# Which engine sums the conditioning products, in what order the weight halves are made, and which products are split in three

## The reference, cut to what matters

```python
for l in range(2):
    mod = (silu(c) @ w_ada[l] + b_ada[l])           # six vectors of 2048: sh1 sc1 g1 sh2 sc2 g2
    h = rms_norm(x) * (1 + sc1) + sh1
    z = h @ w_in[l]     # differential attention q, k, v; latent q_a, kv_a, k_rope; gate u, v
    out_a = diff_attention(...)                     # 6 heads, chunk mask, ALiBi
    out_b = latent_attention(...)                   # 6 heads, through w_uq and w_ukv
    out_c = spatial_gating(...)
    x = x + g1 * (concat(out_a, out_b, out_c) @ w_out[l])
    h = rms_norm(x) * (1 + sc2) + sh2
    x = x + g2 * conv_ffn(h)     # up to 2 x 5632 columns, 3-tap conv, silu gate, down to 2048
```

## Time and profile before

| | |
|---|---|
| three runs | 2524.81, 2528.46 (median), 2529.74 us |
| the profiled execution | 2523.4 us, its span 2521.6 us |
| TensorE matmul busy | 2422.4 us, 96% |
| VectorE busy | 1796.8 us, 71% |
| ScalarE busy | 1122.5 us, 45% |
| GpSimd busy | 536.5 us, 21% |
| granted TensorE clock, mean | 0.975 |

### The profile page before, as it was taken

The page is one execution under the profiler, slowest core; times in us unless marked ns, Lnnn a source line. Parts: engine busy times, 40 slices in busy tenths (PEclk is TensorE's granted clock), DMA queues, the critical chain, the costliest instruction groups (busy, mean ns, idle before and its releaser), DMA issues.

```text
span 2521.6 us, 37553 instructions
## 1 busy us (share of the span) xinstructions
PE 2422.4 (96%) x15080; PEld 2025.7 (80%) x15080; DVE 1796.8 (71%) x2477; ACT 1122.5 (45%) x1549; POOL 536.5 (21%) x565
## 2 busy tenths in 40 slices
PE   6799999989999999999999999999999999999999
PEld 2578778768888888888878888777888888888888
DVE  2455657987668889989986477788766566665765
ACT  2233555345443454445444355534544344443543
POOL 3332310132322133213330120002231002200220
PEclk8899999999999999999999999999999999999999
DMA  9999886677779888898787677556776556555654
GB/s 311 340 300 313 263 265 205 207 244 242 252 257 316 277 257 266 295 297 253 255 267 230 202 234 219 180 170 210 243 247 213 185 187 188 184 187 188 185 185 149
DMA packets 450509, 596.86 MB, mean 237 GB/s; under 512 B 24172, under 2 KB 397984, under 8 KB 450080
## 3 DMA queue, kind: packets, MB, share of 16 engines
q1 hardware_dynamic: 394640, 392.47, 49.1%
q0 software_dynamic: 55296, 201.35, 24.4%
q10 hardware_dynamic: 400, 0.65, 0.1%
HBM read 592.30 MB, written 2.10 MB: 236 GB/s over the span
## 4 chain that ended last, share of the span: by engine, by line
PE 85%; DVE 6%; DMA 3%; issue 3%; ACT 2%; POOL 0%; ACTq 0%; DVEq 0%; SPq 0%; POOLq 0%
PE bank L1029 85%; DMA ada<-in_w_ada_dram 3%; DVE wlo L1594 1%; ACT whi L1351 1%; DVE acc L1588 1%; DVE xT L1632 1%; DMA rows<-in_b_ada_dram 0%; DVE r L1651 0%; DVE T L1666 0%; DVE hx L1687 0%; ACT hx L1418 0%; PE bank L1320 0%; DMA raw<-in_w_in_dram 0%; ACT sq L1404 0%; DVE xT L1633 0%
## 5 line engine op out<-in xcount | busy, mean ns | idle before, releaser
L1029 PE MATMUL bank<-hx,whi 128*128 128x512 f32 (+1 forms) x3968 | 1365.6, 391 | 4.1 <-DVE hx L1689 4.1
L1594 DVE TENSOR_TENSOR wlo<-raw,whi 128x1024 fp32r<-128x1024 f32 (+1 forms) x774 | 936.6, 1216 | 593.9 <-ACT whi L1351 592.6
L1351 ACT ACTIVATE whi<-raw 128x1024 fp32r<-128x1024 f32 (+1 forms) x774 | 785.3, 1019 | 1118.2 <-PE bank L1029 1093.7
L1029 PE MATMUL bank<-hx,wlo 128*128 128x256 f32 x3840 | 1096.5, 286 | 31.2 <-DVE hx L1687 10.8
L1029 PEld LDWEIGHTS bank<-hx,whi 128*128 128x128 f32 x3968 | 744.7, 190 | 165.6 <-DVE hx L1689 4.8
L1029 PEld LDWEIGHTS bank<-hx,wlo 128*128 128x128 f32 x3840 | 733.5, 191 | 62.7 <-issue 25.1
L1029 PE MATMUL bank<-mx,whi 128*128 128x512 f32 x1728 | 618.5, 400 | 0.0
L1029 PE MATMUL bank<-mx,wlo 128*128 128x256 f32 x1728 | 495.5, 287 | 2.7 <-DVE wlo L1594 1.2
L983 POOL DMA_DIRECT2D ada<-in_w_ada_dram x384 | 253.9, 664 | 1135.5 <-DVE acc L1588 581.9
L1029 PEld LDWEIGHTS bank<-mx,whi 128*128 128x128 f32 x1728 | 329.6, 191 | 76.1
L1029 PEld LDWEIGHTS bank<-mx,wlo 128*128 128x128 f32 x1728 | 331.6, 192 | 15.4 <-issue 10.6
(11 more groups left out here) (163 smaller groups left out, 1326.6 us busy)
## 6 DMA issues: line engine op xcount, KB each, us to landing
ada<-in_w_ada_dram POOLq DMA_DIRECT2D x384, 512.0 KB, 6.3
raw<-in_ffn_w_up_dram SPq DMA_DIRECT2D x352, 512.0 KB, 4.5
raw<-in_ffn_w_down_dram SPq DMA_DIRECT2D x176, 512.0 KB, 4.0
raw<-in_w_in_dram SPq DMA_DIRECT2D x128, 512.0 KB, 5.4
raw<-in_w_out_dram SPq DMA_DIRECT2D x48, 512.0 KB, 4.8
raw<-in_w_out_dram SPq DMA_DIRECT2D x32, 256.0 KB, 3.1
raw<-in_mla_w_uq_dram SPq DMA_DIRECT2D x12, 384.0 KB, 4.2
raw<-in_mla_w_ukv_dram SPq DMA_DIRECT2D x6, 512.0 KB, 4.9
```

Source lines behind the costliest of these rows:

```text
L1029: return pe.matmul(out_, lhsT, rhs, start=start, stop=stop, skip_group_check=True)
L1351: return act.activation(out_, in_, ACT.Copy)
L1594: i_ = tt(dst, src, high.bitcast(F32), ALU.subtract)
```

## The change

- `VECTOR_HALVES` replaces `VECTOR_BATCHES`: halves 4, 10 to 19, 22 and 23, that is the first half of batch 2, and batches 5, 6, 7, 8, 9 and 11. Batches 4 and 10 go to TensorE, and so does the second half of batch 2, as before.
- The spreading of batches over slots: batch 1 over 16 slots (was 14); layer 0's batch 2 over 36 slots, then batches 3 and 4 from pair 14 of the late pairs (they were 2, 3 and 4 over 70); layer 1's batch 9 over 36 slots, then batch 10 from pair 10 (they were 9 and 10 over 94).
- `three` in place of `paired` for the w_in pairs 9 to 13 (all that are neither `TWO_PAIRS` nor `TOKEN_PAIRS`), for all of w_out, and for the last pair of the last down pass of each layer. Their `copy` goes to ScalarE; their `addz` and `res` are one VectorE instruction where they were two.
- `place_splits` puts `av`, and `prob` whose `exp` came earlier, between `hi` and `lo`.
- `transition` issues the three products of the norm itself, and one burst between the first and the second, another behind `inv`, if the next batch is TensorE's.
- Small moves in the queues: `dak` in three groups, a free slot ahead of a group in layer 1, the latent items ahead of the gate's in `out_projection` and one empty slot fewer there, `inv` of the latent queries one group earlier.

```diff
-VECTOR_BATCHES = (4, 6, 7, 8, 10)
+VECTOR_HALVES = (4, 10, 11, 12, 13, 14, 15, 16, 17, 18, 19, 22, 23)
+LAST_DOWN = (len(PASS_BLOCKS) - 1, 7)
+TWO_PAIRS = DAQ_PAIRS + DAK_PAIRS
+SPREAD_FROM = (SGV_PAIRS[0], QA_PAIRS[1])
     def vector_next(self):
-        return self.ada_g // 8 in VECTOR_BATCHES
+        return self.ada_g // 4 in VECTOR_HALVES
-                self.ada_over(2, len(order) - 6)
+                self.ada_over(2, len(order) - 4)
...
-        if l == 0:
-            self.ada_over(5, 18 + 30 + 22)
-        else:
-            self.ada_over(11, 28 + 30 + 24 + 12)
+        self.ada_over(3 if l == 0 else 10, 36)
...
+            if pair == SPREAD_FROM[l]:
+                self.ada_over(5 if l == 0 else 11, 4 * len(LATE_PAIRS[LATE_PAIRS.index(pair):]) - 2 + 24 + 10)
...
+        for kind in ("T", "H", "L"):
+            for k in range(2):
+                self.add(kind, l, "kva", k)
         self.steps.extend([("sg", l, 0), ("sg", l, 1), ("Tsg", l, 0), ("Tsg", l, 1)])
...
-        q.extend([[], [("krgain", l)], [("ukvjob", l, 0)] + qa[0],
+        q.extend([[("krgain", l)], [("ukvjob", l, 0)] + qa[0],
...
         self.drain()
+        self.add("ms", l, j, 0)
+        spare = not self.vector_next()
+        if spare:
+            self.burst()
+        self.add("ms", l, j, 14)
+        self.add("ms", l, j, 15)
         self.add("root", l, j)
         self.add("inv", l, j)
-        if not self.vector_next():
+        if spare:
             self.burst()
...
+            steps.extend(own[:n])
+            own = own[n:]
+            ready = [x for x in own if x[0] == "av" or (x[0] == "prob" and ("exp", *x[1:]) not in own)]
+            splits(None, ready)
+            steps.extend(x for x in own if x not in ready)
...
+                            elif x_.what == "win" and x_.i not in TWO_PAIRS:
+                                i_ = three(b[:, 0:S], wh, wl, hi(hx, k), lo(hx, k), start, stop)
                             elif x_.what == "wout":
-                                i_ = paired(b, wh, wl, mixed(k), start, stop)
+                                i_ = three(b[:, 0:S], wh, wl, mixed(k)[:, 0:S], mixed(k)[:, S:2 * S], start, stop)
+                            elif x_.what == "down" and (x_.b, x_.i) == LAST_DOWN:
+                                i_ = three(b[:, 0:S], wh, wl, hi(mx, k), lo(mx, k), start, stop)
...
-                    order.after(stt(xa, b[:, S:2 * S], g, xa, ALU.mult, ALU.add))
+                        if (ph, pair) != LAST_DOWN:
+                            order.after(stt(xa, b[:, S:2 * S], g, xa, ALU.mult, ALU.add))
                     stt(xa, b[:, 0:S], g, xa, ALU.mult, ALU.add).then_inc(emptied_dve, 1)
```

More of the change, by code:

```diff
@@ L361, in projection @@
                 self.queue.extend([[("banks", (0, 1, 2))] + groups[0]] + groups[1:])
-                self.queue.extend([[("dak", l, 0), ("dakmul", l, 0)],
-                                   [("dak", l, 1), ("dakmul", l, 1), ("dak", l, 2), ("dakmul", l, 2)]])
+                self.queue.extend([("dak", l, v), ("dakmul", l, v)] for v in range(3))
                 self.queue.extend(self.heads(l, 0, NH, 3))
-                self.queue.extend(self.stats(l, J_O))
+                self.queue.extend(self.stats(l, J_O) + [[]] * l)
                 self.queue.extend([[("spr", l, v)] + [t for h in (2 * v, 2 * v + 1) for t in
@@ L396, in out_projection @@
                 self.add(kind, l, "sg", g)
-        for kind in ("T", "H", "L"):
-            for k in range(2):
-                self.add(kind, l, "kva", k)
         self.add("banks", (0, 1, 2, 3, 6, 7))
@@ L447, in trunk_squares @@
             self.add("padd", l, j, pair)
-        else:
-            self.queue.append([("ms", l, j, 0), ("ms", l, j, 14), ("ms", l, j, 15)])
     def transition(self, l, what, two):
@@ L526, in place_splits, with splits @@
         steps, split, used = [], 0, 0
-        def splits(limit=None):
+        def splits(limit=None, ready=()):
             nonlocal split
+            ready = list(ready)
             while split < min(limit or used + SPLITS, len(self.units)):
                 steps.append(("hi", split))
+                steps.extend(ready)
+                ready = []
                 steps.append(("lo", split))
                 split += 1
-        for t in self.steps:
+            steps.extend(ready)
+        at = 0
+        while at < len(self.steps):
+            t = self.steps[at]
+            at += 1
             if t[0] == "first":
@@ L538, in place_splits @@
                 continue
-            if t[0] not in self.EVACS and split >= SPLITS:
-                splits()
             steps.append(t)
[L542 to L545, removed]
+            if t[0] not in ("mm", "ukvmm", "uqmm"):
+                continue
+            used = t[1] + 1 if t[0] == "mm" else t[3] + (2 if t[0] == "uqmm" else 1)
+            end = at
+            while end < len(self.steps) and self.steps[end][0] not in ("mm", "ukvmm", "uqmm"):
+                end += 1
+            own = self.steps[at:end]
+            at = end
+            n = 0
+            while n < len(own) and own[n][0] in self.EVACS:
+                n += 1
+            steps.extend(own[:n])
[3 more added lines that the diff above has]
+            steps.extend(x for x in own if x not in ready)
         assert split == used == len(self.units)
@@ L582, in empties @@
         if k in ("copy", "addz"):
-            return ("act" if k == "copy" and t[2] in TOKEN_PAIRS else "dve"), [("win", *t[1:])]
+            return ("act" if k == "copy" and t[2] not in TWO_PAIRS else "dve"), [("win", *t[1:])]
         if k == "res":
@@ L1363, in _ @@
                     i_.then_inc(hi_ready, 1)
-                elif kind == "copy" and t[2] in TOKEN_PAIRS:
+                elif kind == "copy" and t[2] not in TWO_PAIRS:
                     l, pair, c_, ph = t[1:]
@@ L1369, in _ @@
                     b_ = t[1]
[L1370 to L1373, removed]
+                    for d in range(2):
+                        if 2 * b_ + d in VECTOR_HALVES:
+                            act.wait_ge(part_summed, num["asum", (b_, d)] + 1)
+                        else:
+                            act.wait_ge(ada_used, num["part", 32 * b_ + 16 * d + 15] + 1)
                     if b_:
@@ L1600, in _ @@
                     a = ch(z, 2 * pair + c_)
-                    if pair not in TOKEN_PAIRS:
+                    if pair in TWO_PAIRS:
                         order.after(tt(a, b[:, S:2 * S], a, ALU.add))
                     tt(a, b[:, 0:S], a, ALU.add).then_inc(emptied_dve, 1)
-                elif kind == "copy" and t[2] not in TOKEN_PAIRS:
+                elif kind == "copy" and t[2] in TWO_PAIRS:
                     l, pair, c_, ph = t[1:]
```

4 lines of the change are left out of this document (2 added, 2 removed).

## The result

The changed kernel takes 2510.66 us (median of four, 2507.39 to 2512.24) where the kernel before took 2529.10 beside it (2524.81 to 2530.76): ratio 0.9928, 95% interval 0.9911 to 0.9945. The forecast was 2512. The medians differ by 18.4 us, the forecast said 16. The profiled execution took 2509.7 us, 13.7 less than the one before; the sum had said 16.1.

The account below looks back on a forecast made before the run. TensorE work was taken as the bound, with VectorE queues in the two attention stages. Terms sum to -16.1 us: 2523.4 profiled becomes 2507, or 2512 with the median's 5 us difference; range 2496 to 2532.

Parts of the forecast that it names:

- Bursts and sums, -14.9: Conditioning on TensorE: nine bursts fewer that count, -16.8 us, and three new sums, +1.9.
- `three`, +8.3: `three` for `paired` on TensorE: 0.360 us a step against 0.347 in w_in and 0.353 in w_out, +8.3 us.
- The second sweep of layer 0, -9: Layer 0's output projection, second half: VectorE relieved, matmuls become the bound; -9 us, ends -12 and -3.
- Transitions, +1.5: Three transitions: idle time grows from 2.8 to about 4.7 us, lengthening matmuls at 1.2 GHz; +1.5 us.
- Waits elsewhere in attention, -10 + 2 - 1: Attention waits and shorter queues -10 us; batch 9's parts in layer 1's projection +2; easier early weight stream -1.
- the wait of 3.70 ahead of the latent keys: Attention: 3.70 us wait counted among 8.9 us of waits to go, latent items being moved ahead of the gate's.
- larger gain: Rival: all queues go and the passes absorb the parts; -33 us, 2496 us; chance 22%.
- First passes, +7: First feed-forward passes of both layers: VectorE overfull with added parts at 1.21 to 1.38 us; +2.4 to +12.6, taken +7.
- Two of my signs: In the first passes TensorE still above 98% busy; a mean `av` below 1.5 us.
- collide: Rival: VectorE and GpSimd collide in first passes; loss from 1.55 us a part, at 1.73 2539 us; slower 15%.
- the third rival: Hardly any change: attention waits return one step later, about 2528 us; with half kept 2521; chance 18%.

Follow-up runs that it names:

- `three` alone: Kernel before with only the change's products and bank emptying (`three` for `paired`, copies on ScalarE, single `res`): 2516.69 us, 0.9956.
- `paired` in the change: Changed kernel with the products and bank emptying of before put back: 2511.27 us, 0.9927 of the kernel before.
- queue moves alone: Kernel before with only the queue moves of `out_projection`: latent items ahead of the gate's, empty group gone, `inv` one group earlier: 2538.6 us, 1.0042.
- the kernel with the slot put back: Changed kernel with only the empty group ahead of the latent queue restored: 2483.53 us, 0.9827 of the kernel before.
- the run with short products: Changed kernel with GpSimd's gate product cut to 8 columns and its low half replaced by a copy: 2494.1 us, 0.9864 of the kernel before.
- the four matmuls: Kernel before with four float32 matmuls of the sums' form added ahead of layer 1's first down unit: 2518.97 us, 0.9958.
- the places alone: Kernel before with only the new `place_splits` (`av` and ready `prob` between `hi` and `lo`): 2522.18 us, 0.9975.
- the batches back on TensorE: Changed kernel with batches 5 and 11 on TensorE again: 2531.44 us, 1.0016 of the kernel before.
- the halves alone: Kernel before with only the new list of VectorE halves and the new spreading over slots: 2507.6 us, 0.9909.
- the bare pause: Kernel before, TensorE waiting longer ahead of layer 1's first down unit, no matmul added: 2531.07 us, 1.0000, times in two groups.

## Why the prediction was right, and where it wasn't

**Bursts and sums, -14.9.** Right: 1408 records, no burst in the first passes, 12 x 32 fewer.

**`three`, +8.3.** Right in price: in w_out three steps of the change take 368.88 - 367.80 = 1.08 us, 0.360 each. As 0.3594 over longer stretches against 0.351 in the same stages before, 880 steps are 7.5 us.
```profile
367.80 0.40 PE L1056 MATMUL bank<-mx,whi 128*128 128x256 f32 x2
...
368.88 0.28 PE L1056 MATMUL bank<-mx,whi 128*128 128x256 f32 x1
```

**The second sweep of layer 0, -9.** Right, and a little more: stage -5.7 with three bursts (+5.6) and `three` in it, a sum (-0.6) out of it, so about -12, my far end. What I hadn't seen is that either remedy alone would have done: moving batch 4, or `three`.

**Transitions, +1.5.** The stage itself is -2.1. The idle time grew as said (layer 0: 4.5 to 5.7 us), but I costed only the burst. `res` is one instruction for two, so the last two pairs of columns reach the squares a microsecond earlier. (`three` alone shortens the two transitions behind w_out to 7.9 us, and `paired` in the change makes them 8.7 again.) What the +1.5 stood for, matmuls at 1.2 GHz behind the longer gap, falls in the stage behind. The first 10 us of layer 1's first pass, before and after (columns as in the earlier trace rows):
```profile
1752.50:1762.50 10.00, 9.67 (x51) 7.84 (x52) 8.37 (x17) 5.13 (x9) 0.75 (x1) 0.99 0.62 210
```
```profile
1752.30:1762.30 10.00, 9.96 (x46) 8.37 (x47) 7.47 (x15) 4.95 (x8) 0.00 (x0) 0.79 0.14 38
```
The clock is at 0.79 for 0.99, an estimated 2.0 us, and in layer 0 at 0.71 for 0.83, 1.2 us. With them the transitions come to about +1, near the forecast.

**Waits elsewhere in attention, -10 + 2 - 1.** Of the waits that I named, those for the q_a copies and ahead of the latent keys went; of the latent heads' low halves only the 0.76 us in the first sweep went, and the 2.4 in layer 1's second sweep stayed. ScalarE's copies brought the one of 3.4. And the step "the wait of 3.70 ahead of the latent keys, for which the latent items are moved" was wrong: I counted the move as a gain and named as its only cost that the product comes 1.4 us earlier. The wait passed to the second job's fourth product. The queue moves alone cost 11 us in the kernel before; in the changed kernel the slot by itself costs 27. The other moves were not tried one by one. The term came out near its value because the rest gave more than I took. Over both attention stages bursts (+9.4), sums (-0.6) and `three` (+7.1) would be +15.9; measured are +3.4. That is -12.5 of stalls and clock against -18 forecast, with a loss of about 29 in the two first sweeps inside it, by the kernel with the slot put back. So relief of VectorE, places and the other moves together are worth over 40 us there, more than my "larger gain" gave them. How they share it isn't shown.

**First passes, +7.** The mis-sized step. Bursts and sums make each pass 11.8 us shorter, measured 3.9 and 3.5: a loss of 16.2 us in two passes. Of these 3.2 are the clock behind the transitions, and 13.0 are left, a little beyond my end of 12.6; 11.2 us of TensorE's waits for `wlo` stand in them. Two of my signs say the same: TensorE is busy for 97% of these passes, not over 98, and a part takes more than 1.5 us. The step took 1.448 - 0.07 = 1.38 for a part, the mean from passes in which VectorE was at 85% and 17 of 90 parts overlapped a two-operand product of GpSimd's. In the first passes 11 of 30 do. There a part measures 1.53 (1.46 on the same footing), and the low halves, which I left at their old price, went from 1.27 to 1.36. My own table had a `lo` of 1.62 beside a product; it wasn't carried into the sum. The rival "collide" named this mechanism; its break-even, 1.55 for a part, wasn't reached. The Trainium skill (SBUF — State Buffer, "SBUF: two separate sides") gives the exclusion that stands behind it; the run with short products agrees, with parts at 1.34 and low halves at 1.26.

**What no step held: -10.** Layer 1's last part runs the same matmuls, but for the last pair of columns, and takes 10 us less. Without it the change would have taken about 2521, which is the third rival with half of the waits kept. The forecast is right partly by luck: +6 in the passes, +5 in attention and +2 in the rest of layer 0 stand against this -10.

## What to carry to other kernels

When an engine is to be filled above some 90%, price every instruction on it anew, not only the added one, and take collisions at the rate of a full engine. A slot that looks empty in a hand-written order may be what gives a product a free bank: move it alone, and compare which bank each product takes and who empties it. When a stage without an edit changes, compare the distance from start to start in it before giving the difference to the edit.

## What the runs showed of the hardware

**Two paces of one stream.** A step of `paired` takes one of two times, with the granted clock at 1.00 in both. The kernel before, time line of TensorE, rows 12 steps apart, twice:
```profile
1959.67 0.40 PE L1029 MATMUL bank<-mx,whi 128*128 128x512 f32 x1
1963.91 0.40 PE L1029 MATMUL bank<-mx,whi 128*128 128x512 f32 x1
...
2299.93 0.40 PE L1029 MATMUL bank<-mx,whi 128*128 128x512 f32 x1
2304.17 0.40 PE L1029 MATMUL bank<-mx,whi 128*128 128x512 f32 x1
```
The same kernel with the four matmuls, of which the first row is the record:
```profile
1955.77 0.64 PE L1029 MATMUL bank<-acc,onez 128*32 128x256 f32 x8
...
1959.68 0.39 PE L1029 MATMUL bank<-mx,whi 128*128 128x512 f32 x1
1963.85 0.39 PE L1029 MATMUL bank<-mx,whi 128*128 128x512 f32 x1
...
2299.76 0.39 PE L1029 MATMUL bank<-mx,whi 128*128 128x512 f32 x1
2303.92 0.39 PE L1029 MATMUL bank<-mx,whi 128*128 128x512 f32 x1
```
4.24 / 12 = 0.353 against 4.16 / 12 = 0.347 us, 1.9%. A pace holds for hundreds of microseconds: the kernel before is in the longer one from 1929 to 2462 us, until the first transposes of the result, and the changed kernel in the shorter one from 1930, both in each of their two traces. Where I followed it, it changed where something else came between: a sum, a burst, a stall. The longer pace in this part had also the kernels with `three` alone, with the places alone, with the queue moves alone and with the batches back on TensorE; the shorter had the halves alone, `paired` in the change, the slot and the short gate. So every trace with batch 11's bursts in layer 1's first pass has the longer pace behind it, unless the four matmuls or the stall came between, and every trace with its sums there the shorter. It isn't a rule for sums, though I expected it to be one: in the kernel before, the sum at 1098 us is followed by steps of 0.353, and bursts are followed by either. The run times of the kernel with the bare pause, in two groups whose means lie 11 us apart, suggest that there the pace differs from one execution to the next. That a break can change it is shown; which of the two it picks, and why, stays open. The 0.347 of the earlier trace rows and the 0.353 of the earlier trace rows, which I had taken for the prices of an up part and of w_out, are by their size the two paces.

**A full VectorE beside GpSimd.** In the first passes the mean part took 1.53 us with 512-column products on GpSimd and 1.34 without, the low half 1.36 and 1.26; one by one, a part beside such a product took 1.92 against 1.28, a low half 1.87 against 1.22. Without these products the kernel took some 16 us less.
